# A two-layer block on one core: power and inverse from one product, state sums kept in their banks, and another order of the second tile's projections

## What is computed

```python
def step(state, inp):
    r_t, w_t, k_t, v_t, kk_t, a_t = inp
    sa = jnp.einsum('bhij,bhj->bhi', state, -kk_t)
    state = (state * w_t[:, :, None, :]
             + sa[..., None] * (kk_t * a_t)[:, :, None, :]
             + v_t[..., None] * k_t[:, :, None, :])
    y_t = jnp.einsum('bhij,bhj->bhi', state, r_t)
    return state, y_t

q = rms_norm(q, q_norm_g)
k = rms_norm(k, k_norm_g)
...
s_own = (jnp.einsum('bhqd,bhkd->bhqk', qi, k_own).astype(f32) * scale
         - slopes[:, None, None] * (tq[:, None] - kpos_own[None, :]))
s_own = jnp.where(kpos_own[None, :] <= tq[:, None], s_own, -jnp.inf)
prob = jax.nn.softmax(s, axis=-1)
```

## Time and profile before

| | |
|---|---|
| median of 3 runs | 2022.75 us |
| lowest, highest | 2019.68, 2024.13 us |
| the profiled execution's own time | 2023.09 us |
| its span | 2021.4 us |
| TensorE, VectorE, ScalarE, GpSimd busy | 86%, 46%, 24%, 14% |
| mean granted TensorE clock | 0.925 |
| DMA | 772.96 MB, 382 GB/s over the span |
| chain that ended last | PE 53%, DMA 27%, DVE 8%, ACT 4% |

### The profile page before, as it was taken

How to read it: one execution, slowest core, us unless ns; L and a number is a source line. 1 busy time by engine, 2 the same in 40 slices (tenths; PEclk the granted TensorE clock), 3 DMA queues, 4 the chain that set the end, 5 groups by cost and what they waited for, 6 DMA issues and landing times.

```text
span 2021.4 us, 31289 instructions
## 1 busy us (share of the span) xinstructions
PE 1739.9 (86%) x12352; PEld 812.8 (40%) x12352; DVE 931.1 (46%) x1995; ACT 478.7 (24%) x1198; POOL 288.6 (14%) x286
## 2 busy tenths in 40 slices
PE   7999987666688968768878999999999999999997
PEld 6888554111145534317763333333333323323322
DVE  4755878788555756755342232232222223223222
ACT  1111434334345433533211110111011101101100
POOL 1000433334442444430000000000000000000000
PEclk9999998666689989878888999999999999999999
DMA  9982999999999999999326999999999999999997
GB/s 390 387 361 92 386 421 421 421 421 421 421 410 421 399 407 377 421 390 370 127 111 245 421 422 422 421 422 422 422 422 422 422 422 422 422 422 422 422 421 308
DMA packets 107064, 772.96 MB, mean 382 GB/s; under 512 B 12148, under 2 KB 12404, under 8 KB 13272
## 3 DMA queue, kind: packets, MB, share of 16 engines
q1 hardware_dynamic: 69408, 500.51, 60.0%
q0 software_dynamic: 36864, 268.45, 32.3%
q10 hardware_dynamic: 696, 2.66, 0.3%
HBM read 770.53 MB, written 1.05 MB: 382 GB/s over the span
## 4 chain that ended last, share of the span: by engine, by line
PE 53%; DMA 27%; DVE 8%; ACT 4%; issue 3%; SPq 3%; POOL 0%; ACTq 0%; DVEq 0%; POOLq 0%
DMA ring<-in_expert_uv,arena 15%; PE psum L2260 14%; DMA ring<-in_w_gate_up 13%; PE psum L2290 8%; PE psum L1869 6%; PE psum L1721 5%; SPq L613 3%; PE psum L1826 2%; PE psum L2302 2%; PE psum L1971 2%; DVE ring L1288 2%; PE psum L1804 1%; PE psum L1910 1%; PE psum L1789 1%; PE psum L2164 1%
## 5 line engine op out<-in xcount | busy, mean ns | idle before, releaser
L2260 PE MATMUL psum<-ring,arena 128*64 128x512 f32 x2048 | 458.5, 597 | 23.8 <-DMA ring<-in_w_gate_up 22.2
L1869 PE MATMUL psum<-ring,arena 64*64 64x512 f32 x2048 | 347.2, 763 | 137.5 <-ACT arena L845 133.2
L1288 DVE CUSTOM_DVE_ANT_0 ring<-ring,arena 128x1024 f32<-128x1024 f32 x256 | 312.3, 1225 | 176.0 <-DMA ring<-in_expert_uv,arena 170.6
L712 POOL DMA_INDIRECT ring<-in_expert_uv,arena x256 | 278.3, 1087 | 600.4 <-PE psum L1869 392.7
L2260 PEld LDWEIGHTS psum<-ring,arena 128*64 128x64 f32 x2048 | 138.8, 137 | 339.1 <-issue 257.0
L2290 PE MATMUL psum<-ring,arena 128*64 128x512 f32 x992 | 219.7, 595 | 0.6
L1666 DVE TENSOR_SCALAR arena<-psum 128x512 f32<-128x512 f32 x32 | 22.1, 692 | 400.6 <-PE psum L2260 400.6
L1869 PEld LDWEIGHTS psum<-ring,arena 64*64 64x64 f32 x2048 | 64.7, 154 | 340.8 <-ACT arena L845 306.7
L1001 ACT ACTIVATE arena<-arena 128x512 f32<-128x512 f32 x32 | 20.2, 632 | 760.5 <-DVE arena L1666 760.5
L836 ACT ACTIVATE arena<-arena 128x1 f32<-128x1 f32 x256 | 51.9, 203 | 319.8 <-DVE arena L1288 316.2
L2290 PEld LDWEIGHTS psum<-ring,arena 128*64 128x64 f32 x992 | 68.5, 137 | 131.9 <-issue 123.9
(11 more groups left out here) (350 smaller groups left out, 1602.9 us busy)
## 6 DMA issues: line engine op xcount, KB each, us to landing
ring<-in_w_gate_up SPq DMA_DIRECT2D x256, 1024.0 KB, 24.7
ring<-in_w_down SPq DMA_DIRECT2D x124, 1024.0 KB, 24.3
ring<-in_stream SPq DMA_DIRECT2D x91, 1024.0 KB, 13.4
ring<-in_expert_uv,arena POOLq DMA_INDIRECT x256
arena<-in_w_down SPq DMA_DIRECT2D x4, 1024.0 KB, 5.9
mats<-in_mats ACTq DMA_DIRECT2D x1, 1152.0 KB
xres<-in_x SPq DMA_DIRECT2D x2, 512.0 KB, 4.2
arena<-in_rows ACTq DMA_DIRECT2D x2, 512.0 KB, 7.7
```

Source lines behind the costliest of these rows:

```text
L712: pool.indirect_dma_start(ring[:, G_SLOTS[b], :], None, expert_uv, bass.IndirectOffsetOnAxis(peer_i[:, tt, k:k + 1], 0)).then_inc(row_in[b ...
L1288: dve.tensor_tensor_reduce(u, u, h2[tt], 1.0, 0.0, ALU.mult, ALU.add, peer_h[:, tt, k:k + 1]).then_inc(dot_done, 1)
L1869: last = pe.matmul(psum[o:o + 64, 6 * tt + h, :], diag[rows, c % 4, :], rows_of[b][rows, 1, h * 512:(h + 1) * 512], start=(k == 0), stop=( ...
L2260: last = pe.matmul(psum[CAP * h:CAP * h + CAP, gu, :], x, w[:, at:at + 512], start=False, stop=(kt == GU_CHUNKS - 1), skip_group_check=True)
```

## The change

**One product for power and inverse.** The matrix and the inverse lie side by side in one tile, si. At levels 2 and 3 one product with the transposed power as the stationary side gives both the next power and the inverse's increment (64 columns for 32); level 1 makes only the power, levels 4 and 5 only the inverse. The inverse lags a level, so there are five levels and no inv steps. z2 moves beside the transposed tok as az, so that wu is one product of 128 columns instead of two of 64.

**States.** fg leaves all its matmuls unfinished in its banks; st adds phi times the state onto the increment in the same bank, and one multiply by the decay on VectorE makes the state. gam and its copies go. fg's banks, the banks of y and the value bank move.

**Order.** Queries and keys come ahead of values in both tiles. In tile 1 the chunks are streamed and projected as six of the mixer, four of queries and keys, two of the mixer, two of values. msq waits for two evictions instead of three. The list ORDER and the slots are new; aff stands directly behind bon on VectorE, prob is cut in two halves of four heads, and attention's later steps stand among the powers.

```diff
@@ -54,11 +54,12 @@
...
+V_BANK = (4, 5)
...
-FG_BANK = (4, 5, 1, 2)
-ST_BANK = 3
...
-Y_BANK = (4, 5, 0, 1)
+FG_BANK = (4, 5, 2, 3)
...
+Y_BANK = (0, 1, 4, 5)
@@ -83,7 +84,7 @@
-MB_ORDER = (4, 5, 0, 1, 2, 3)
+MB_ORDER = (0, 1, 2, 3, 4, 5)
@@ -98,7 +99,7 @@
...
-        seq += rw + mb if tt else mb + rw
+        seq += rw[:6] + mb[:4] + rw[6:] + mb[4:] if tt else mb + rw
@@ -166,23 +167,22 @@
...
-          "exp": 27, "prob": 28, "mturn0": 30, "mturn1": 31, "att": 33,
+          "exp": 27, "prob0": 28, "prob1": 28, "mturn0": 30, "mturn1": 31, "att": 33,
...
-          "gram0": 42, "gram1": 43, "nt": 44, "aff": 64, "z1": 62, "wu": 63, "gam0": 69, "gam1": 70, "q2": 73, "yp": 75,
-          "ys": 79, "ln1": 86, "ln2": 88, "ln3": 89, "norm2": 97, "turn4": 100, "route": 102}
+          "gram0": 42, "gram1": 43, "nt": 44, "aff": 40, "z1": 64, "wu": 65, "phi0": 71, "phi1": 72, "q2": 78, "yp": 79,
+          "ys": 82, "ln1": 88, "ln2": 90, "ln3": 91, "norm2": 99, "turn4": 102, "route": 104}
...
-    for lv in range(1, 5):
+    for lv in range(1, 6):
...
-        at["inv%d" % lv] = 44 + 4 * lv
...
-        at["fg%d" % c] = 65 + c
-        at["st%d" % c] = 71 + 2 * c
-        at["om%d" % c] = 82 + c
-        at["or%d" % c] = 91 + c
+        at["fg%d" % c] = 67 + c
+        at["st%d" % c] = 73 + 2 * c
+        at["om%d" % c] = 84 + c
+        at["or%d" % c] = 93 + c
@@ -191,10 +191,9 @@
...
-rw5.0 rw5.1 exps mixr kmod rw6.0 rw6.1 rkk rw7.0 bonus rw7.1 mixv gup kk mb0.0 mb0.1 tilde mb1.0 mb1.1 bon mb2.0 mb2.1 mb3.0 mb3.1
-tok mb4.0 mb4.1 gram0 gram1 mb5.0 nt mb5.1 msq pow1 msum rms inv1 pow2 qk inv2 mscore0 pow3 mscore1 inv3 soft pow4 exp inv4 aff z1
-wu fg0 fg1 fg2 fg3 gam0 prob st0 mturn0 gam1 st1 mturn1 q2 st2 att yp st3 om0 ys om1 ln1 om2 ln2 om3 ln3 or0 or1 or2 or3 norm2 turn4
-route""".split()
+rw5.0 rw5.1 exps mixr kmod mb0.0 mb0.1 mb1.0 mb1.1 mb2.0 mb2.1 rkk mb3.0 mb3.1 msq rw6.0 rw6.1 msum rms rw7.0 bonus qk rw7.1 mixv gup kk
+mscore0 mb4.0 tilde mb4.1 mscore1 bon mb5.0 aff soft mb5.1 tok exp gram0 gram1 nt pow1 prob0 pow2 prob1 mturn0 pow3 mturn1 pow4 att pow5
+om0 z1 om1 wu fg0 fg1 fg2 fg3 phi0 om2 st0 phi1 st1 om3 st2 q2 yp st3 ys ln1 ln2 ln3 or0 or1 or2 or3 norm2 turn4 route""".split()
@@ -850,10 +847,11 @@
...
-                for q, dst in enumerate((mv[:, tt, :].rearrange("p (a t) -> p a t", a=4), mq[tt], mk[:, :, a:b])):
+                for q, dst in enumerate((mq[tt], mk[:, :, a:b], mv[:, tt, :].rearrange("p (a t) -> p a t", a=4))):
...
-                    act.copy(dst, psum[:, MBANK[tt][q % 2], :].rearrange("p (a t) -> p a t", a=4)).then_inc(mb_out, 1)
+                    bank = MBANK[tt][q] if q < 2 else V_BANK[tt]
+                    act.copy(dst, psum[:, bank, :].rearrange("p (a t) -> p a t", a=4)).then_inc(mb_out, 1)
@@ -1296,7 +1295,7 @@
...
-                dve.wait_ge(mb_out, 3 * (tt + 1))
+                dve.wait_ge(mb_out, 3 * tt + 2)
@@ -1321,12 +1320,14 @@
...
-                yield "prob"
-                dve.wait_ge(mexp_out, NH * (tt + 1))
-                ordered(dve.reciprocal(mx[:, 1, :], mx[:, 1, :]))
-                for h in range(NH):
-                    ins = dve.tensor_scalar(sc[tt][:, h, :], sc[tt][:, h, :], mx[:, 1, h:h + 1], None, ALU.mult)
-                ins.then_inc(prob_ready, 1)
+                for par in range(2):
+                    yield "prob%d" % par
+                    hs = slice(4 * par, 4 * par + 4)
+                    dve.wait_ge(mexp_out, NH * tt + 4 * par + 4)
+                    ordered(dve.reciprocal(mx[:, 1, hs], mx[:, 1, hs]))
+                    for h in range(4 * par, 4 * par + 4):
+                        ins = dve.tensor_scalar(sc[tt][:, h, :], sc[tt][:, h, :], mx[:, 1, h:h + 1], None, ALU.mult)
+                    ins.then_inc(prob_ready, 1)
@@ -1462,6 +1463,19 @@
...
+                yield "aff"
...
+                dve.wait_ge(tilde, tt + 1)
+                dve.wait_ge(sig_out, 9 * tt + 9)
...
@@ -1485,43 +1499,30 @@
...
-                def heads(bank):
-                    return psum[:, bank, 0:T].rearrange("p (h t) -> p h t", h=NH)
...
-                for lv in range(1, 5):
+                for lv in range(1, 6):
...
+                    dve.wait_ge(ps_mm, 5 * tt + lv)
+                    w = 2 * CL if lv in (2, 3) else CL
+                    out = psum[:, 0, 0:NH * w].rearrange("p (h t) -> p h t", h=NH)
...
-                        dve.wait_ge(ps_mm, 3 * tt + lv)
-                        dve.tensor_copy(pw_s[tt] if lv % 2 else gr[tt][:, 0, :, 0:CL], heads(0)).then_inc(ps_out, 1)
-                    yield "inv%d" % lv
-                    dve.wait_ge(ix_mm, 4 * tt + lv)
-                    dve.tensor_tensor(inv[tt], inv[tt], heads(4), ALU.add).then_inc(ix_out, 1)
-                yield "aff"
...
...
+                        dve.tensor_copy(si[tt][:, :, 0, :], out[:, :, 0:CL]).then_inc(ps_out, 1)
+                    if lv > 1:
+                        dve.tensor_tensor(si[tt][:, :, 1, :], si[tt][:, :, 1, :], out[:, :, w - CL:w],
+                                          ALU.add).then_inc(ix_out, 1)
...
-                dve.tensor_copy(z2[tt], psum[:, 0, :].rearrange("p (h c) -> p h c", h=NH)).then_inc(wu_out, 1)
+                dve.tensor_copy(az[tt][:, :, 1, :], psum[:, 0, :].rearrange("p (h c) -> p h c", h=NH)).then_inc(wu_out, 1)
...
-                    yield "gam%d" % j
+                    yield "phi%d" % j
...
-                    f, g = (psum[:, b0:b0 + 2, T * i:T * i + T].rearrange("p b (c j) -> p b c j", c=4) for i in range(2))
+                    f = psum[:, b0:b0 + 2, 0:T].rearrange("p b (c j) -> p b c j", c=4)
...
-                    dve.tensor_copy(gam[tt][:, 2 * j:2 * j + 2, :, :], g).then_inc(fg_out, 1)
@@ -1534,12 +1535,9 @@
...
-                        nx = states[g + 1]
...
-                        dve.wait_ge(fg_out, 4 * tt + 2 * (c // 2) + 2)
-                        ordered(dve.tensor_tensor(nx, psum[:, ST_BANK, g % 2 * T:g % 2 * T + T].rearrange("p (a i) -> p a i", a=4),
-                                                  gam[tt][:, c, :, :], ALU.add))
-                        dve.tensor_tensor(nx, nx, pl[:, :, g:g + 1].to_broadcast([P, 4, HD]), ALU.mult).then_inc(st_out, 1)
+                        dve.tensor_tensor(states[g + 1], psum[:, FG_BANK[c], T:2 * T].rearrange("p (a i) -> p a i", a=4),
+                                          pl[:, :, g:g + 1].to_broadcast([P, 4, HD]), ALU.mult).then_inc(st_out, 1)
@@ -1891,7 +1889,7 @@
...
-                    half = psum[:, MBANK[tt][p // 2 % 2], (p % 2) * CW:(p % 2 + 1) * CW]
+                    half = psum[:, MBANK[tt][p // 2] if p < 4 else V_BANK[tt], (p % 2) * CW:(p % 2 + 1) * CW]
@@ -1912,7 +1910,7 @@
...
-                pe.wait_ge(mb_out, 3 * (tt + 1))
+                pe.wait_ge(mb_out, 3 * tt + 2 if tt else 3)
@@ -1931,7 +1929,7 @@
...
-                    pe.wait_ge(prob_ready, tt + 1)
+                    pe.wait_ge(prob_ready, 2 * tt + par + 1)
@@ -2020,6 +2018,8 @@
...
+                    if i == 0 and tt:
+                        pe.wait_ge(mb_out, 3 * TT)
@@ -2041,48 +2041,49 @@
...
-                def within(bank, lhs, rhs, w, off=0, pitch=None):
+                def within(bank, lhs, rhs, w):
...
-                        at = h * (pitch or w) + off
+                        b, at = bank + h * w // W2, h * w % W2
...
-                            last = pe.matmul(psum[ts, bank, at:at + w], lhs[ts, h, :], rhs[ts, h, :], start=True, stop=True)
+                            last = pe.matmul(psum[ts, b, at:at + w], lhs[ts, h, :], rhs(ts, h), start=True, stop=True)
...
-                for lv in range(1, 5):
-                    s_src = gr[tt][:, 0, :, 0:CL] if lv % 2 else pw_s[tt]
-                    t_src, t_dst = (nts[tt], pw_t[tt]) if lv % 2 else (pw_t[tt], nts[tt])
+                power, inverse, both = (lambda ts, h: si[tt][ts, h, 0, :], lambda ts, h: si[tt][ts, h, 1, :],
+                                        lambda ts, h: si[tt][ts, h, :, :])
+                begun = lambda ts, h: gr[tt][ts, 0, h, 0:CL]
+                for lv in range(1, 6):
+                    s_src = si[tt][:, :, 0, :] if lv > 1 else gr[tt][:, 0, :, 0:CL]
+                    t_src = (pw_t, nts)[lv % 2][tt]
...
-                        pe.wait_ge(ps_out, 3 * tt + lv - 1)
...
-                    within(2, s_src, t_src, CL).then_inc(pt_mm, 1)
-                    if lv < 4:
-                        within(0, t_src, s_src, CL).then_inc(ps_mm, 1)
-                    yield "inv%d" % lv
-                    pe.wait_ge(pt_out, 4 * tt + lv)
-                    if lv > 1:
-                        pe.wait_ge(ix_out, 4 * tt + lv - 1)
-                    within(4, t_dst, inv[tt], CL).then_inc(ix_mm, 1)
...
-                v_tok = tok[tt][:, 3, :].rearrange("p (h c) -> p h c", h=NH)
-                a_tok = tok[tt][:, 0, :].rearrange("p (h c) -> p h c", h=NH)
+                        pe.wait_ge(ps_out, 3 * tt + min(lv - 1, 3))
+                    if lv < 5:
```

(38 more changed lines are left out.)

34 lines of the change are left out of this document (16 added, 18 removed).

## The result

The changed kernel takes 2032.93 us (median of six runs, 2031.47 to 2034.91) where the kernel before takes 2022.66 beside it: the ratio is 1.0051, with a 95% interval of 1.0038 to 1.0065. It is slower by 10.3 us. I had forecast 2022.2 with a range up to 2031.5. The profiled execution of after took 2034.91 us with a span of 2033.1.

What follows compares the result with a forecast made beforehand. Expert loop and gather were taken as bound by DMA streaming, the second tile by its chain of waits. Second tile +3.2 and gather -3.8 gave -0.6 on the profiled 2023.09, about 2022.2 us; range 2013.5 to 2031.5.

Steps and rivals of the forecast that it cites:

- The reading of the generators: Second tile: the list only merges generators, so mixv to bon queue behind qk; tok may start at 996.2, before 972.42.
- the values' pair: Second tile's two value projection chunks on TensorE, ahead of msum: 8.79 us, ending at 979.6.
- From tok over aff, soft and the copies to pow1: Second tile: VectorE's aff, soft and tok copies 5.9 us, then gram1, nt and masks 2.9; pow1 starts at 1005.0.
- pow1 to fg: Second tile's powers, inverse and attention steps: 768 records in 21 us, between 16.5 and 27.3; fg starts at 1026.
- by blocks: Price of pow1 to fg by instruction refill: six blocks of 128 records at 3.6 us each, 21.6 us.
- by the array: Price of pow1 to fg by TensorE's array work: 27.3 us at half clock, some 16 at full clock.
- fg to the reciprocal: Second tile's states through ln: fg to last ys eviction 16 us instead of 22, ln1 and ln2 1.7 earlier.
- its rewarming: TensorE getting warm again before the second tile's last output product: 0.7 us, bounds 0 and 3.4.
- Second tile in all: Net change of the second tile's chain: +3.2 us, from -1.3 to +9.5.
- The gather: First tile's hole before wu, 4.9 us of DMA lost, mostly closes: -3.8 us, from -6 to 0.
- The rival that came: Second tile: VectorE's queue behind qk, TensorE cold through the powers, pow1 to fg 27; 2031.5 us, chance 0.27.
- The first rival: Second tile: refill and clock kinder, pow1 to fg 17, no refill in the states; 2015 us, chance 0.28.

Runs made afterwards that it cites:

- e2: Changed kernel with TensorE's norm sums and scores and ScalarE's norm really ahead of the value projection in the second tile: 2021.87 us.
- e3: Changed kernel with qk moved behind tok in the second tile's order list, scores and exponentials among the powers: 2023.37 us.
- e5: Changed kernel with 16 useless 128x512 products in TensorE's holes in the second tile, behind msum, the score products, ln1 and ln2: 2025.35 us.
- e7: e2 with attention's four output products (om) moved back among the states, ahead of ys and behind ln1 and ln2: 2017.64 us.
- e8: Kernel before with only the states' sums left open in fg's banks, one VectorE multiply per state, no gam: 2023.3 us.
- e11: Kernel before with ten useless 128x512 products at the second tile's end, from ahead of the output product to the first front gather: 2016.62 us.
- e6: Changed kernel with the second tile's last inverse product issued three times, 128 records more, same result: 2033.1 us.
- e4: Kernel before with only VectorE's aff moved directly behind bon in both tiles: 2020.72 us.
- e10: Changed kernel with ten useless 128x512 products only at the second tile's end, none in its earlier holes or at ln1: 2030.18 us.
- e12: Kernel before with states' sums left open and aff directly behind bon, power and inverse still separate products: 2019.44 us.

## Why the prediction was wrong

**The reading of the generators held.** qk ahead of mixv, VectorE idle until ScalarE's Exp, tok behind bon: predicted 985.1 for qk and 996.2 for tok, measured 982.67 and 993.49. 1.6 of the 2.5 between is the values' pair, which I took at 8.79 and which ran in 7.17 at full clock. From tok over aff, soft and the copies to pow1 8.8 were predicted, 8.3 measured. e2 and e3 show that this queue is what costs: some 10 us less without it.

**The step that failed first: pow1 to fg, 21 predicted, 26.5 measured.** The count of 768 records was right. (The list of the nine products names six narrow ones where there are seven; the 10.3 us are those of seven.) I had set two prices against each other, 21.6 by blocks and 16 to 27.3 by the array, and took 21 near the first, as if the one hid the other. They add: 20.4 of work, which lies between the two ends, 4.6 of stalls, 1.5 of handovers. The clock was in part to blame as well, by an amount that no run separates: it was 0.50 up to 1008, then 1.00 in 1012 to 1028. At that full clock two of the stalls stand, 1.49 and 1.87. That the stalls are the refill of instructions is inferred from their spacing of 128 records and from the earlier trace rows; no run shows a fetch itself. The Trainium skill ("Runtime: NRT & Kernel Launch", "Instruction fetch mechanics") calls crossing a block mostly hidden; the trace disagrees for stretches of small products (4.6 of 26.5 us) and agrees where long products stand ahead (from 1017.82 to the end of wu, no stall).

**The step that failed second, and cost most: fg to the reciprocal.** I had 5.8 less up to ys and 1.7 less at ln, 20.5 for 28.0; it was 28.2. In e5, with its stalls moved and TensorE at full clock up to ys, the stretch takes 21.0. So the count of the removed work was right to about 1 us (21.0 has 0.7 of stall and a cold ln1 in it, 20.5 had 2 of stall), and what I left out was the clock of what remains. I had priced "its rewarming" at 0.7 for the output product alone, with a bound of 3.4, and had not applied it to ys, ln1, ln2 and om2. Of the 7.7 missed, 1.8 are stalls (2.10 and 1.65, where I had 2 in all), and 4.8 the slower array: 1.7 in ys, 2.0 in ln1 and ln2, 1.1 in om2. The output product, where I had looked for it, lost nothing (34.2 from the reciprocal on, for 34.4).

What the removed work had done for the clock is shown in part. The turns and the attention ran at half clock themselves, so it was not they that kept the array fast; from om0 on it was fast, with an om product behind ys and one behind each of ln1 and ln2. Two windows of before, over turns and attention and from om0 to behind ln2:

```profile
1022.00:1031.00 9.00, 8.85 (x130) 7.85 (x132) 3.63 (x8) 2.02 (x2) 0.00 (x0) 0.50 0.02 4
...
1032.00:1046.00 14.00, 12.95 (x236) 10.07 (x232) 5.62 (x8) 2.56 (x3) 0.00 (x0) 1.00 0.49 180
```

e7 against e2 shows that the om products behind ln1 and ln2 hold the clock there. For om2 and ys the timelines show only that the clock fell behind the stalls; whether turns and attention would have covered these stalls no run tests.

**Second tile in all:** 3.2 predicted; 2.4 more up to fg (12.4 for 10.0), 7.7 more behind it, less the 0.7 for rewarming that did not come, give 12.6; measured 12.4.

**The gather: -3.8 predicted.** The mechanism is there: 420 GB/s instead of 217 in the hole. From the issue of pick 168 (counted from 0) to that of the last one the three kernels that keep the hole (before, e8, e11) take 223.6 to 225.2 us, and the other eleven 218.7 to 223.1. Over all picks these three take 699 to 700, the others 694 to 701, on the mean 2.6 less; a single kernel says nothing, since the changed one has 699.6 in its profile and the kernel before 699.9. In the total it is some 2 at most: 12.4 lost in the second tile and 10.3 in the whole. The size of this term is not settled better than 0 to 4.

**The rival that came.** It is the third, a blocked queue run cold, at 2031.5 against 2032.9. It decided where it said, pow1 to fg over 25 us. Its mechanism was only half right: the cold in the powers ended at 1008, the stalls made up the rest of their excess, and the larger loss to the clock came behind fg. Its price was an end of my range, with no room for its own error; a range that ends on a rival's point leaves out half of that rival. With the upper bounds that the prediction itself gives (27.3 for the powers, 3.4 for the rewarming, 0 for the gather) it would have reached 2035.0. The first rival, refill and clock kinder, fell by the four stalls.

## What to carry to other kernels

When work is moved out of a chain, ask what it kept warm and what it gave time for: the work removed behind fg was counted right to about 1 us and gave nothing back, because TensorE then stood between its steps, with its stalls bare, and ran most of them at half clock. A list of names that merges generators is not the order: read on each engine which step waits first, and what is queued behind it. And two costs of the same stretch, instruction stalls and array time, are added unless a row shows one under the other. A shift of 18 records moved the stalls of this kernel by microseconds, so an edit that adds or removes matmuls also has to be read for where they fall.

## What the runs showed of the hardware

- The half clock costs small products less than large ones. 116 records of 32x32 take 1.81 us at 0.50 and 122 take 1.26 at 1.00, 15.6 and 10.3 ns each; the sixteen records of tok's transposes take 3.67 in after and 1.91 in before, nearly twice.
- Useless products can be worth their place: ten of them in waits of 4 us and 1 us give 5.7 us in the kernel before, with an interval from 3.6 to 7.9. Nine ahead of the powers did not warm these: in e5 the clock was 0.50 again at 996, 8 us behind the last of them and behind a hole of 2.92 us.
- Stalls without a semaphore come at positions 128 records apart and move with the program: 18 records ahead of pow1 moved all of them (e5). 128 records more don't add one at its full price: five sum to 4.74 us, where four sum to 4.62 (e6).
- TensorE's granted clock can fall with the engine busy throughout: in before the values' pair takes 8.79 us instead of 7.17, with no hole ahead of it. It did so in before and e4 (8.74), and the clock fell there in e11 too, but not in after, e8, e10 and e12 (7.17). What decides it I did not find; it is worth 1.6 us ahead of tok.
